# A two-block network in fp32r terms: hi and lo side by side for 512-column matmuls, modulation rows spread, first state loads moved

## The chip, the cores and the metric

The kernel runs on one core of a Trainium2 chip. It has five engines that run side by side and meet at semaphores: TensorE (matmuls, PE in the profile, its weight loads PEld), VectorE (DVE), ScalarE (ACT), GpSimd (POOL) and SyncE (SP), which here issues the transfers of the weights. Matmuls write PSUM, eight banks of 512 fp32 columns on 128 partitions. The metric is the device time of one execution in microseconds (us); less is better.

## The reference, cut to what matters

Two blocks over 256 positions of width 2048. The first has adaptive norms (a modulation of six times 2048 values, from c), a token mixer and a feed-forward part; the second has a sliding window attention, a state space model and a merge.

```python
mod = (silu(c) @ ada_w + ada_b)            # sh1, sc1, g1, sh2, sc2, g2
h = rmsnorm(x, norm1_g) * (1 + sc1) + sh1
z = h @ w_in                               # q, 6 x kv, gates, lx, ly, ga, gb
o_a = nsa_attention(...)                   # compressed, selected, window
o_b = gelu(ly) * rg_lru(causal_dwconv(lx))
merged = sigmoid(ga) * (o_a @ proj_a) + sigmoid(gb) * (o_b @ proj_b)
x = x + g1 * (merged @ w_out)
h = rmsnorm(x, norm2_g) * (1 + sc2) + sh2
gate, val = split(h @ ffn_up)
x = x + g2 * ((gelu(causal_dwconv(gate)) * val) @ ffn_down)
x = rmsnorm(x, final_g)
# second block: h @ w_in_2 -> attention, s5_ssm, glu; merged @ w_out_2, added to x
```

All of it is fp32 to begin with. The big products are made of three fp32r terms.

## The kernel before

**Groups and units.** The work of TensorE is a list of groups (`groups()`), each a product of an input with 512 columns of a weight: kc, vc, k, v, gates, q, lx, ly, then four times ga, gb, pa, pb, then wout, and for each half of the feed-forward part six gate and val and four down; behind these the groups of the second block (q2, kv2, u2, ag2, z2, ga2, pa2, gs2, gluA, gluB, ps2, wout2). A group has two units per slot, eight in most, twelve in down. A unit is a load of 2 x 128 weight rows by 512 columns, 512 KB.

**Terms.** Each input lies in SBUF as hi (rounded to fp32r) and lo (the rest), made by `put_pair`: all of hi, and all of lo behind it. For each unit ScalarE rounds the weights into whi (L1267) and VectorE writes the rest over the raw ones as wlo (L1272). TensorE then makes, for each of two rows and four output blocks, three matmuls of 256 columns into pairs[g % 2] (L1792): whi with hi, whi with lo, wlo with hi. Groups of mode N (v) swap the roles, with 512 columns (L1798).

**PSUM.** Two pairs of two banks take the groups in turn; four more banks (bank, states_in) belong to the mixers. When a group is done `evac` takes its pair out, and gives it back with the semaphore freed; the group after next waits for it.

**Order.** Every engine walks the same list of units (`walk`): at unit u VectorE and ScalarE split unit u + 4 and then do the steps of the jobs that stand at u: the evacuation of the group before, and the mixers compress, nsa (attention), lru, recurrence_back, ssm_tables, make_turns, output_factors, attention2 and states. A job gives its engine steps between which it hands over by semaphores. Whatever waits on an engine holds up what is written behind it there.

**Modulation rows.** A row is 128 of the 12,288 modulation values: 1 MB of weights, which takes two of the ten places of the ring wraw, and one VectorE instruction over 2048 elements (`ada`, L1248). Rows 0 to 31 come first; the others stand behind slots of groups, as `g.ada[s]` says; the row of slot s follows the split of unit 2s + 1, which is at step u = 2s - 3 of the walk.

**Norms.** Ahead of gate0 and of q2 the pipeline is flushed and `norm2` or `last_norms` runs; `normed_rest` then makes h2 or h3 in blocks of two rows, one ahead of each unit.

**States.** The job states (from ag2(0), unit 1) has GpSimd load turns and bz (`load_turns` L1082, `load_bz` L1085) and TensorE make states_in with bz (L1097).

## Time and profile before

| | |
|---|---|
| time, median of 3 runs | 2693.28 us (2691.06 to 2696.19) |
| time of the profiled execution | 2692.64 us |
| its span, first to last instruction | 2690.9 us |
| granted TensorE clock, mean | 0.984 |
| busy: PE, PEld, DVE, ACT, POOL | 2597.1, 2505.2, 1877.7, 1107.6, 227.3 us |
| moved | 568.13 MB, mean 211 GB/s |

The profile is of one execution. A granted clock of 1.00 is 2.4 GHz, one of 0.50 is 1.2 GHz. A matmul's duration in it is its way through the array; how fast matmuls follow each other is read from their starts. Groups of rows below name a line of the kernel before, the engine, the operation, and the tile written and the tiles read.

### The profile page before, as it was taken

How to read it: one execution, taken by the hardware profiler on the slowest of the kernel's cores; microseconds unless marked ns; L12 is line 12 of the kernel's file. 1: busy time of each engine (PE TensorE's matmuls, PEld its weight loads, DVE VectorE, ACT ScalarE, POOL GpSimd, SP SyncE). 2: the span in 40 equal slices, each digit the busy share in tenths (PEclk: the TensorE clock that was granted, in tenths of full speed). 3: DMA queues.
4: the chain of work that ended last, by engine and by line, in shares of the span. 5: the costliest groups of instructions: out<-in, count | busy, mean ns of one | idle time of the engine just before them, and what ended most of it. 6: DMA issues, size and time to landing. Idle time of an engine off the chain costs nothing.

```text
span 2690.9 us, 48148 instructions
## 1 busy us (share of the span) xinstructions
PE 2597.1 (97%) x20256; PEld 2505.2 (93%) x20256; DVE 1877.7 (70%) x2519; ACT 1107.6 (41%) x1381; POOL 227.3 (8%) x190
## 2 busy tenths in 40 slices
PE   7999999989999999899999999999999999999999
PEld 5789999889999999899999999999999888899999
DVE  7865667676866674679976556654487898898563
ACT  1033456455333344444443344444444444534432
POOL 0000000000000001000466610001100000000000
PEclk9988999999999999999999999999999999999999
DMA  9974466456888886478866766665555554465664
GB/s 404 424 269 151 156 204 188 142 157 212 274 268 275 278 276 211 134 254 274 278 225 212 221 211 181 183 185 180 165 181 180 157 162 132 149 189 176 195 197 134
DMA packets 243462, 568.13 MB, mean 211 GB/s; under 512 B 17424, under 2 KB 21520, under 8 KB 228784
## 3 DMA queue, kind: packets, MB, share of 16 engines
q1 hardware_dynamic: 233776, 530.33, 60.9%
q0 software_dynamic: 9472, 34.74, 3.6%
q8 instruction: 160, 2.62, 0.4%
q14 instruction: 54, 0.44, 0.1%
HBM read 550.85 MB, written 14.16 MB: 210 GB/s over the span
## 4 chain that ended last, share of the span: by engine, by line
PE 75%; DVE 12%; DVEq 4%; DMA 3%; ACT 3%; issue 2%; SPq 0%; ACTq 0%; POOL 0%
PE pair L1792 65%; DVE wlo L1272 4%; DMA wraw<-ada_wT_dram 3%; ACT whi L1267 2%; DVE wraw L1248 1%; PE pair L1365 1%; PE bank L499 1%; PE pair L1798 1%; DVEq L338 1%; PE pair L1785 1%; PE states_in L684 1%; PE bank L1365 1%; PE states_in L1370 1%; PE states_in L1097 0%; PE pair L1803 0%
## 5 line engine op out<-in xcount | busy, mean ns | idle before, releaser
L1272 DVE TENSOR_TENSOR wlo<-wraw,whi 128x1024 fp32r<-128x1024 f32 x777 | 977.6, 1267 | 586.0 <-ACT whi L1267 559.5
L1267 ACT ACTIVATE whi<-wraw 128x1024 fp32r<-128x1024 f32 x777 | 813.4, 1057 | 1163.9 <-PE pair L1792 669.7
L1792 PE MATMUL pair<-h_hi,whi 128*128 128x256 f32 x3936 | 1136.3, 289 | 22.2 <-DVE h_lo L426 9.2
L1792 PE MATMUL pair<-h_lo,whi 128*128 128x256 f32 x3936 | 1121.5, 285 | 0.0
L1792 PE MATMUL pair<-h_hi,wlo 128*128 128x256 f32 x3936 | 1120.8, 285 | 0.0
L1792 PEld LDWEIGHTS pair<-h_hi,whi 128*128 128x128 f32 x3936 | 763.6, 194 | 41.5 <-issue 34.9
L1792 PEld LDWEIGHTS pair<-h_lo,whi 128*128 128x128 f32 x3936 | 763.9, 194 | 0.6
L1792 PEld LDWEIGHTS pair<-h_hi,wlo 128*128 128x128 f32 x3936 | 763.1, 194 | 0.0
L1248 DVE SCALAR_TENSOR_TENSOR wraw<-wraw,cb 128x2048 f32<-128x2048 f32 x96 | 221.4, 2309 | 58.1 <-DMA wraw<-ada_wT_dram 56.8
L1792 PE MATMUL pair<-hid_hi,whi 128*128 128x256 f32 x768 | 218.5, 284 | 0.0
L1792 PE MATMUL pair<-hid_hi,wlo 128*128 128x256 f32 x768 | 217.3, 283 | 0.0
L1792 PE MATMUL pair<-hid_lo,whi 128*128 128x256 f32 x768 | 217.3, 283 | 0.0
L1792 PEld LDWEIGHTS pair<-hid_lo,whi 128*128 128x128 f32 x768 | 147.4, 192 | 0.2
L1792 PEld LDWEIGHTS pair<-hid_hi,whi 128*128 128x128 f32 x768 | 147.4, 192 | 0.2
L1792 PEld LDWEIGHTS pair<-hid_hi,wlo 128*128 128x128 f32 x768 | 147.4, 192 | 0.0
L1792 PE MATMUL pair<-m_hi,whi 128*128 128x256 f32 x512 | 145.5, 284 | 0.0
L1792 PE MATMUL pair<-m_lo,whi 128*128 128x256 f32 x512 | 144.9, 283 | 0.0
L1792 PE MATMUL pair<-m_hi,wlo 128*128 128x256 f32 x512 | 144.9, 283 | 0.0
L1792 PEld LDWEIGHTS pair<-m_lo,whi 128*128 128x128 f32 x512 | 98.3, 192 | 0.1
L1792 PEld LDWEIGHTS pair<-m_hi,whi 128*128 128x128 f32 x512 | 98.3, 192 | 0.1
L1792 PEld LDWEIGHTS pair<-m_hi,wlo 128*128 128x128 f32 x512 | 98.3, 192 | 0.0
L1365 PEld LDWEIGHTS pair<-h_f,wfour 128*128 128x128 f32 x256 | 49.1, 195 | 29.0 <-issue 22.6
(443 smaller groups left out, 3296.5 us busy)
## 6 DMA issues: line engine op xcount, KB each, us to landing
wraw<-w_in_dram SPq DMA_DIRECT2D x312, 512.0 KB, 3.7
wraw<-ada_wT_dram SPq DMA_DIRECT2D x96, 1024.0 KB, 5.8
wraw<-ffn_up_dram SPq DMA_DIRECT2D x192, 512.0 KB, 3.7
wraw<-ffn_down_dram SPq DMA_DIRECT2D x96, 512.0 KB, 4.6
wraw<-w_out_dram SPq DMA_DIRECT2D x64, 512.0 KB, 4.6
wfour<-w_in_dram SPq DMA_DIRECT2D x16, 1024.0 KB, 13.5
wraw<-proj_a_dram SPq DMA_DIRECT2D x32, 512.0 KB, 5.3
wraw<-proj_b_dram SPq DMA_DIRECT2D x32, 512.0 KB, 4.9
```

The costliest lines, as they stand in the source:

```text
L338: return ve.drain() if self.me == "dve" else None
L499: ins = te.matmul(bank[1][:, 0, 0:60], wcmp[which][:, l, :], blocks[:, l, :], start=(l == 0), stop=(l == 31))
L684: te.matmul(bank[3][:, 0, :], vv(br, 0), pt[:, br, 0:T], start=False, stop=False, skip_group_check=True)
L1248: ve.scalar_tensor_tensor(out=row, in0=row, scalar=1.0, in1=cb[:, :], op0=ALU.mult, op1=ALU.mult, accum_out=mod[:, col:col + 1]).then_inc( ...
L1267: sc.activation(whi[:, r, 0:w], wraw[:, PLACE[z], 0:w], ACT.Copy).then_inc(hi_ready, 1)
L1272: ve.tensor_tensor(wlo[:, PLACE[z], 0:w], wraw[:, PLACE[z], 0:w], whi[:, r, 0:w].bitcast(F32), ALU.subtract).then_inc(lo_ready, 1)
L1365: ins = te.matmul(out, w[:, g * CB + o * P:g * CB + (o + 1) * P], x, start=(c == 0 and o % 2 == 0), stop=(c == DC - 1), skip_group_check=True)
L1370: ins = te.matmul(flat(bank[2 + b][:, :, :]), x[:, b * P:(b + 1) * P], w[:, 3 * CB:4 * CB], start=(c == 0), stop=(c == DC - 1))
L1785: ins = te.matmul(pair[:, 2 * b, 0:48], x[:, b * P:(b + 1) * P], w[:, k * 48:(k + 1) * 48], start=(k == 0 and t == 0), stop=(k == 15 and t ...
L1792: ins = te.matmul(pair[:, o, :], w[:, at_w + o * P:at_w + (o + 1) * P], x, start=(k == 0 and o % 2 == 0 and t == 0), stop=(k == last and t ...
L1798: ins = te.matmul(flat(pair[:, 2 * b:2 * b + 2, :]), x[:, b * P:(b + 1) * P], w[:, at_w:at_w + CB], start=(k == 0 and t == 0), stop=(k == ...
```

## The change

- `put_pair` puts hi and lo of each row of 256 next to each other, so that a row of both is 512 columns. The parts are still to be had apart.
- The eight PSUM banks are now two sets of four (wides); pairs[n] is the first half of set n, the mixers' banks are the other halves.
- 41 groups are marked wide: from pb0 to down3 of the first half, without the wout groups, and gate0 to val5 of the second half. In a wide group TensorE makes, for each row and output block, one matmul of whi with 512 columns (hi and lo) into a whole bank and one of wlo with hi into its first 256 columns.
- The evacuation of a wide group begins with a ScalarE copy of the second halves into a new tile tl and a VectorE add of the first halves; what follows reads tl and not PSUM. For gates made by ScalarE alone, those who need them wait for ScalarE's semaphore.
- Modulation rows: the four of k1 and v1 go to unit pair 3 of lx0 to lx3. Of the sixteen in gate1 to val4 of the first half (two in each), four go to wout0 (two), wout1 and wout2, and twelve are one each, at slot 2, in gate0 to val5.
- A job first_turns loads the first two turns and bz in q2's first group; the job states no longer does.
- ctmp and ob_f lie elsewhere, and the last part of the recurrence is split from lr.

```diff
     def put_pair(name, at, n):
-        return put(name + "_hi", at, [P, n, T], F32R), put(name + "_lo", at + n * 1024, [P, n, T], F32R)
+        both = put(name, at, [P, n, 2, T], F32R)
+        return both[:, :, 0, :], both[:, :, 1, :], both
...
-    at = [(out[of(kind, 1)], s) for kind in ("k", "v") for s in (1, 3)]
-    at += [(out[of("q", i)], 1) for i in range(4)] + [(out[of(kind, i)], 1) for i in range(4) for kind in ("lx", "ly")]
+    at = [(out[of("q", i)], 1) for i in range(4)] + [(out[of("ly", i)], 1) for i in range(4)]
+    at += [(out[of("lx", i)], s) for i in range(4) for s in (1, 3)]
...
-    at = [(out[of(kind, i)], s) for i in range(1, 5) for kind in ("gate", "val") for s in (1, 3)]
+    at = [(out[of("wout", i)], s) for i, s in ((0, 1), (0, 3), (1, 1), (2, 1))]
+    at += [(out[of(kind, i)], 2) for i in range(6) for kind in ("gate", "val")]
...
+    for g in range(of("pb", 0), of("down", 3, 0) + 1):
+        out[g].wide = out[g].kind != "wout"
+    for g in range(of("gate", 0, 1), of("val", 5, 1) + 1):
+        out[g].wide = True
...
-    pairs = [ctx.enter_context(nc.psum_tensor(f"pair{n}", [P, 4, T], F32)) for n in range(2)]
+    wides = [ctx.enter_context(nc.psum_tensor(f"banks{n}", [P, 4, 2, T], F32)) for n in range(2)]
+    pairs = [w[:, 0:2, :, :].rearrange("p b c t -> p (b c) t") for w in wides]
...
+    def first_turns(j):
+        j.sync("to_pool", "dve", "pool", j.drained())
+        if j.me == "pool":
+            po.wait_ge(pe_units, U1[of("down", 3, 1)])
+            po.wait_ge(turns_out, 256)
+            for n in range(2):
+                load_bz(n)
+                load_turns(n)
+        yield
...
+        if gr.wide:
+            e, w = tl, wides[g % 2]
+            yield from j.hand("to_act", "dve", "act", j.drained())
+            if computed("act"):
+                ins = sc.activation(tl[:, :, :], w[:, :, 1, :], ACT.Copy)
+            yield from j.hand("act_to_dve", "act", "dve", ins)
+            if me == "dve":
+                done(ve.tensor_tensor(tl[:, :, :], w[:, :, 0, :], tl[:, :, :], ALU.add))
+                ve.drain()
+            done = lambda ins: ins
...
+    job(first_turns, start_of("q2", 0) + 2)
     job(states, start_of("ag2", 0) + 1, end_of("gs2", 3) - 2)
...
+                if gr.wide:
+                    for o in range(4):
+                        out, cols = wides[g % 2][:, o, :, :], slice(at_w + o * P, at_w + (o + 1) * P)
+                        te.matmul(out, wh[:, cols], X[gr.x][2][:, k, :, :], start=(k == 0), stop=(k == last),
+                                  skip_group_check=True)
+                        ins = te.matmul(out[:, 0, :], wl[:, cols], hi[:, k, :], start=False, stop=(k == last),
+                                        skip_group_check=True)
```

VectorE behind the prologue, where k1 is split and the first compress is prepared. L1272 is the split, L1248 a modulation row, L490 the additions that fill blocks. Before:

```order
L1272 TENSOR_TENSOR wlo<-wraw,whi 128x1024 x2
L1248 SCALAR_TENSOR_TENSOR wraw,mod<-wraw,cb 128x2048
L1272 TENSOR_TENSOR wlo<-wraw,whi 128x1024
L1416 COPY k_71<-bank 128x512 x2
L1416 COPY v_72<-states_in 128x512 x2
L1272 TENSOR_TENSOR wlo<-wraw,whi 128x1024 x3
L1248 SCALAR_TENSOR_TENSOR wraw,mod<-wraw,cb 128x2048
L490 TENSOR_SCALAR blocks<-kc_73,vec 128x60 x8
```

And now (the split is L1290, the additions L502):

```order
L1290 TENSOR_TENSOR wlo<-wraw,whi 128x1024 x3
L1446 COPY k_64<-banks 128x512 x2
L1446 COPY v_65<-banks 128x512 x2
L1290 TENSOR_TENSOR wlo<-wraw,whi 128x1024 x3
L502 TENSOR_SCALAR blocks<-kc_66,vec 128x60 x8
```

Two rows are gone from ahead of the additions; the splits and copies stand in the same order.

VectorE at the start of gate0 of the first half, where the second norm is applied block by block (L403 and L426; a split between them). Before:

```order
L1272 TENSOR_TENSOR wlo<-wraw,whi 128x1024
L403 SCALAR_TENSOR_TENSOR t_70<-res,scA,rstd 128x256 x2
L426 SCALAR_TENSOR_TENSOR h_lo<-t_70,mod,h_hi 128x256 x2
L1272 TENSOR_TENSOR wlo<-wraw,whi 128x1024
L403 SCALAR_TENSOR_TENSOR t_69<-res,scA,rstd 128x256 x2
```

And now (L415, L438; a modulation row is L1266):

```order
L1290 TENSOR_TENSOR wlo<-wraw,whi 128x1024
L415 SCALAR_TENSOR_TENSOR t_63<-res,scA,rstd 128x256 x2
L438 SCALAR_TENSOR_TENSOR h_53<-t_63,mod,h_53 128x256 x2
L1290 TENSOR_TENSOR wlo<-wraw,whi 128x1024
L1266 SCALAR_TENSOR_TENSOR wraw,mod<-wraw,cb 128x2048
L415 SCALAR_TENSOR_TENSOR t_62<-res,scA,rstd 128x256 x2
```

A modulation row stands between the second split and the third block.

GpSimd at the start of the second block. Before:

```order
L1612 DMA outT_dram<-res 128x16x256
L1082 DMA turns_101<-turns_scratch 128x1024
L1085 DMA bz<-B_dram 128x256
L1082 DMA turns_102<-turns_scratch 128x1024
L1085 DMA bz<-B_dram 128x256
```

And now:

```order
L1098 DMA bz<-B_dram 128x256
L1095 DMA turns_94<-turns_scratch 128x1024
L1098 DMA bz<-B_dram 128x256
L1095 DMA turns_95<-turns_scratch 128x1024
L1648 DMA outT_dram<-res 128x16x256
```

The four loads stand ahead of the store of outT, bz first.

## Rows read from the trace of the kernel before

**Rows 1.** The page, part 1 (busy time, share, instructions) and part 4 (chain, by engine).

```profile
PE 2597.1 (97%) x20256; PEld 2505.2 (93%) x20256; DVE 1877.7 (70%) x2519; ACT 1107.6 (41%) x1381; POOL 227.3 (8%) x190
...
PE 75%; DVE 12%; DVEq 4%; DMA 3%; ACT 3%; issue 2%; SPq 0%; ACTq 0%; POOL 0%
```

**Rows 2.** Windows: length, busy PE, PEld, DVE, ACT, POOL, PEclk, DMA share, GB/s.

```profile
700.00:1000.00 300.00, 300.00 (x2502) 300.00 (x2502) 202.94 (x175) 115.89 (x112) 0.00 (x0) 1.00 0.82 274
...
1291.50:1317.60 26.10, 23.50 (x195) 23.15 (x193) 25.15 (x28) 8.48 (x8) 11.17 (x7) 1.00 0.74 247
...
1340.70:1386.80 46.10, 46.10 (x387) 46.10 (x386) 36.38 (x30) 19.76 (x21) 32.01 (x20) 1.00 0.73 236
```

**Rows 3.** Timeline of PE in down3, 256 columns: start, duration, what.

```profile
1499.80 0.28 PE L1792 MATMUL pair<-hid_hi,whi 128*128 128x256 f32 x1
...
1507.96 0.28 PE L1792 MATMUL pair<-hid_hi,wlo 128*128 128x256 f32 x1
```

**Rows 4.** Timeline of PE in v1, 512 columns.

```profile
195.36 0.39 PE L1798 MATMUL pair<-whi,h_hi 128*128 128x512 f32 x1
...
199.90 0.39 PE L1798 MATMUL pair<-wlo,h_hi 128*128 128x512 f32 x1
```

**Rows 5.** Groups of DVE (700:1000, then 1317:1400): count, busy, mean ns; ScalarE's timeline.

```profile
L1248 DVE SCALAR_TENSOR_TENSOR wraw<-wraw,cb 128x2048 f32<-128x2048 f32 x26 | 59.6, 2292 | 41.0 <-DMA wraw<-ada_wT_dram 40.8
L1452 DVE TENSOR_TENSOR res<-t,pair 128x1024 f32<-128x1024 f32 x4 | 4.9, 1215 | 0.0
...
L1272 DVE TENSOR_TENSOR wlo<-wraw,whi 128x1024 fp32r<-128x1024 f32 x34 | 53.0, 1588 | 10.9 <-ACT whi L1267 10.0
...
2030.43 1.01 ACT L1429 ACTIVATE u<-pair 128x1024 f32<-128x1024 f32 x1
```

**Rows 6.** The first compress: timelines of DVE and PE, pieces of the chain, windows.

```profile
159.62 2.29 DVE L1248 SCALAR_TENSOR_TENSOR wraw<-wraw,cb 128x2048 f32<-128x2048 f32 x1
...
171.24 1.11 PE L499 MATMUL bank<-blocks,wcmp 128*128 128x60 f32 x4 [3.57 <-DVEq L338]
...
171.24 13.91 PE bank L499 x64
185.15 6.70 PE pair L1798 x24
...
234.29 7.09 PE bank L499 x64
...
171.00:187.00 16.00, 15.76 (x69) 15.37 (x70) 7.71 (x8) 2.18 (x3) 0.00 (x0) 0.50 0.01 5
...
234.00:242.00 8.00, 8.00 (x74) 8.00 (x73) 0.00 (x0) 0.58 (x2) 0.00 (x0) 1.00 0.60 215
```

**Rows 7.** The first states: a piece of the chain, the timeline of PE, a window.

```profile
2032.69 5.42 DMA bz<-B_dram
...
2038.25 2.08 PE L1097 MATMUL states_in<-u,bz 32*128 32x256 f32 x8 [3.13 <-DMA bz<-B_dram]
...
2038.00:2044.00 6.00, 5.75 (x25) 5.03 (x26) 3.43 (x5) 0.00 (x0) 0.00 (x0) 0.50 0.36 143
```

**Rows 8.** Timeline of PE in gate4 of the first half.

```profile
1311.12 0.36 PE L1792 MATMUL pair<-h_hi,whi 128*128 128x256 f32 x1 [2.15 <-DVE wlo L1272]
```

**Rows 9.** Timelines of DVE and PE in gate0 of the first half.

```profile
1105.37 1.22 DVE L1272 TENSOR_TENSOR wlo<-wraw,whi 128x1024 fp32r<-128x1024 f32 x1 [0.95 <-ACT whi L1267]
...
1109.34 1.23 DVE L1272 TENSOR_TENSOR wlo<-wraw,whi 128x1024 fp32r<-128x1024 f32 x1 [0.95 <-ACT whi L1267]
...
1116.38 0.39 PE L1792 MATMUL pair<-h_hi,whi 128*128 128x256 f32 x1 [0.62 <-DVE h_lo L426]
```

**Rows 10.** Timelines of DVE in lx1 and of PE in q3 and lx3.

```profile
399.62 0.42 DVE L346 CAST oa_hi<-states_in 128x256 fp32r<-128x256 f32 x1 [3.79 <-PE bank L598]
...
469.67 0.39 PE L584 MATMUL bank<-ident,pc 128*15 128x128 f32 x2 [2.31 <-DVE pc L575]
...
568.21 0.39 PE L584 MATMUL bank<-ident,pc 128*15 128x128 f32 x2 [0.18 <-DVE pc L575]
```

More of the change, by code:

```diff
@@ L50, in __init__ @@
         self.flush = False
+        self.wide = False
 def groups():
@@ L154, in build_program @@
     q4 = (put("q4a", z2 + 20 * K, [P, 4, T]), put("q4b", z2 + 24 * K, [P, 4, T]))
-    ob_f = put("ob_f", z2 + 16 * K, [P, DC, T])
+    ob_f = put("ob_f", z2 + 20 * K, [P, 12, T])
     lr = put("lr", rM, [P, 4, T])
@@ L216, in build_program @@
     b1 = put("b1", off, [P, DC])
-    ctmp = put("ctmp", off, [P, 4, 256])
+    ctmp = put("ctmp", z1 + 28 * K, [P, 4, 256])
+    tl = put("tl", off, [P, 4, T])
     bz = put("bz", off, [P, 2, 2, P])
@@ L782, in recurrence_back @@
                     j.eng.wait_ge(lru_in, 48)
-                ins = split(ob, 4 * b, 4, ob_f[:, 4 * b:4 * b + 4, :])
+                if b == 3:
+                    ve.drain()
+                ins = split(ob, 4 * b, 4, ob_f[:, 4 * b:4 * b + 4, :] if b < 3 else lr[:, :, :])
             j.ready["ob"].append(j.give("to_pe", "dve", ins))
@@ L1115, in state_outputs @@
         return j.give("pe_to_dve", "pe", ins)
+    def first_turns(j):
[7 more added lines that the diff above has]
+        yield
     def states(j):
         me, ins = j.me, None
-        j.sync("to_pool", "dve", "pool", j.drained())
-        if me == "pool":
-            po.wait_ge(turns_out, 256)
-            for n in range(2):
-                load_turns(n)
-                load_bz(n)
         if me == "dve":
@@ L1428, in evac @@
                 dst, src = ends()
-                done(sc.activation(dst, src, f))
+                ins = done(sc.activation(dst, src, f))
+            if gr.wide:
+                j.ready[k] = j.give("act_to_dve", "act", ins)
         elif k in ("lx", "gate"):
@@ L1448, in evac @@
         elif k == "pa":
-            if me == "dve":
+            if GR[of("ga", i)].wide:
+                j.take("act_to_dve", "dve", j.ready["ga"])
+            elif me == "dve":
                 j.eng.wait_ge(*evacuated("ga", i))
@@ L1454, in evac @@
         elif k == "pb":
-            if me == "dve":
+            if GR[of("gb", i)].wide:
+                j.take("act_to_dve", "dve", j.ready["gb"])
+            elif me == "dve":
                 j.eng.wait_ge(*evacuated("gb", i))
@@ L1788, in unit @@
                 k, at_w = 2 * n + kk, kk * CB
-                if "T" in gr.mode:
+                if gr.wide:
+                    for o in range(4):
[4 more added lines that the diff above has]
+                                        skip_group_check=True)
+                elif "T" in gr.mode:
                     for o in range(4 if gr.mode == "T" else 2):
```

15 lines of the change are left out of this document (7 added, 8 removed).

## The prediction, made before the changed kernel ran

> **What bounds the kernel now.** I read the page's busy table and its chain first: TensorE is busy for 97% of the span and holds 75% of the chain [rows 1]. A busy TensorE need not be at its peak, so next come the stretches: from 700 to 1000 us it never pauses, at full clock, while VectorE works 203 of 300 us and ScalarE 116 [rows 2]. The timeline then gives the pace there. From 1499.80 to 1507.96 us lie 68 starts of 256-column matmuls, 8.16 / 68 = 0.120 us each [rows 3]; a unit (two rows of 128 weights, four output blocks, three terms: 24 matmuls) takes 2.88 us. In the blocks pb0 to pb3 and gate1 to val3 of the first half, in the downs and in the whole second half, every unit takes exactly that, so whatever the change saves on TensorE there reaches the end, unless another engine's work then comes last.
>
> The rest of the time goes in places of a few us each: a wait and a slow clock near 170 us [rows 6], the mixers from 254 to 622 us, the two norms, one stall at 1309 us [rows 8], the first states at 2035 us [rows 7]. The change touches five of them.
>
> **The wide matmuls.** Thirteen groups from pb0 to pb3 (104 units), twelve gate and val groups and four downs of the first half (96 + 48) and twelve gate and val groups of the second (96): 344 units. In each unit eight triples (hi, lo, and hi with the low weights: 3 x 256 columns) become eight pairs, one 512-column matmul over hi and lo and one of 256 columns. The columns are the same, 768; one matmul and one weight load fewer. The trace has 512-column matmuls of the same type in v1: 20 starts from 195.36 to 199.90 us, 0.227 us each [rows 4]. A triple costs 0.360, a pair 0.227 + 0.120 = 0.347, so 0.013 us x 8 x 344 = 36 us. Nothing in v1 mixes the two widths, so 30 to 38 goes into the range.
>
> The rows put 256 further columns at 0.227 - 0.120 = 0.107 us, so each matmul has 0.013 us beyond its columns, and that is what one matmul fewer saves [rows 3, 4]. The Trainium skill speaks against the size of this ("TensorE: Matmul & The Clock Gate", Back-to-back issue gap): the gap is N/2.4 + 2.5 ns, so a matmul fewer would bring 2.5 ns, an estimate of 7 us for the 2752 pairs, and the sum would end at 2671. The trace does not agree: 0.120 us for 256 columns, not 0.109.
>
> What the wide form adds: per group a ScalarE copy of 1024 elements out of PSUM, 1.01 us, and a VectorE add from PSUM of 1.22 us [rows 5]; 41 groups, 41 and 50 us. They lie beside the matmuls. From 700 to 1000 us VectorE has 15.6 us of work per group of 23; it becomes 16.8 in 22.2. The pair of banks is given back two units into the next group and is wanted six units later. No group is short of cover except where ssm_tables and make_turns run.
>
> **That tight stretch.** From 1291.5 to 1317.6 us (gate4) VectorE is busy 25.2 of 26.1 us and TensorE stands 2.15 us for a split weight (the group takes 26.1 instead of 8 x 2.88 = 23.0, 3.0 us more) [rows 2, 8]. The change takes one modulation row of two out of each group from gate1 to val4 (2.3 us [rows 5], more while GpSimd works) and adds 1.2 us, so VectorE gains 1.1 us a group where TensorE is faster by 0.85: over the seven groups to gate4 some 2 to 4 us of lead more, as much as the stall. I count 3.0 us gained. In gate5 and val5 it goes the other way: split subtracts take 1.59 us there because GpSimd is busy, against 1.23 elsewhere [rows 5, 9]; two rows at 2.3 x 1.59 / 1.23 = 3.0 and two adds make 36.4 + 6.0 + 2.4 = 44.8 us of work for 44.4 us [rows 2]. That lasts two groups; the bounds are -3 and +6 us.
>
> **The first modulation rows.** k1 and v1 lose their four rows. Now the row at 159.62 us, which waited for a transfer, stands ahead of the 32 block additions; TensorE starts on them at 171.24 us, after 3.57 us idle [rows 6]. Behind that the clock stands at 0.50 from 171 to 187 us: the 64 compress matmuls take 13.91 us, and the same 64 later, at clock 1.00, take 7.09 [rows 6]. The next 24 matmuls of v1 take 6.70 instead of 24 x 0.227 = 5.45. Without the two rows ahead of them (2 x 2.3 us of VectorE, and their transfers) the additions are ready 4.6 us sooner, at 166.6, and TensorE wants them at 171.24 - 3.57 = 167.67. Then the clock should hold, as it does in the second compress, where nothing is waited for. Sum 3.57 + 6.82 + 1.25 = 11.6. Bounds: 3, if the clock falls all the same, and 13, if the first units of v1 get their weights sooner too.
>
> Four rows go to the second half of the groups lx0 to lx3 (steps at unit 3). In lx1 VectorE waits 3.79 us for TensorE right behind that place [rows 10]; the same wait stands in lx0 and lx2, and each covers a row of 2.3. In lx3 there is no such wait: the row stands ahead of the compressed scores, for which TensorE waits 0.18 us now [rows 10], and 2.5 us then. In q3 the same step, behind such a row, waits 2.31 us [rows 10]. I take +3, bounds 0 and 9.2 (four rows uncovered).
>
> **The rows of the feed-forward.** Four go to wout0 to wout2, where TensorE leads by nothing and VectorE has half its time free: nothing. One goes into gate0, where the second norm is still being applied: VectorE and ScalarE hand blocks over in steps of 3.97 us (the splits at 1105.37 and 1109.34 us) and TensorE already waits 0.62 us for h_lo [rows 9]. 2.3 us in that chain come through whole, and an idle time of 3 us stands before a low clock elsewhere [rows 6, 7]: +3.5, bounds 2 and 5. GpSimd's load of cz waits for the last row, now val5's; nobody wants cz before the third gate group of the second half, over 200 us later.
>
> **The states' first loads.** GpSimd issues turns and bz at 2032 us, behind a drain of VectorE; bz lands 5.42 us after its issue and TensorE idles 3.13 us, then runs 6.0 us at clock 0.50 with 5.75 busy [rows 7]. In the new order they are issued in q2's first group, ahead of the spill, a whole group and more sooner. The idle time goes, and about half of the 5.75: -6.0, bounds -3.1 and -6.5. The spill of outT comes behind them on GpSimd's queue, which costs it the issue of four transfers, some 2 us, with tens of us to spare. What is late next is the state chain itself, unchanged.
>
> **Costs I set at nothing.** hi and lo now interleave (rows of 256, 1 KB apart): casts and ScalarE writes have a strided target. If the cast lost its fast form it would cost VectorE half a microsecond in a dozen groups, under cover. The mixers' banks are the other half of the same eight and are not used in the wide blocks. The number of bytes is unchanged; 274 GB/s becomes 284.
>
> **The sum** against the profiled execution, 2692.6 us (its median differs by 0.6): -36 - 3 - 11.6 + 3 + 3.5 - 6 = -50.1, so 2642.5.
>
> **The rivals.**
> 1. The clock falls at the first compress all the same, or the additions stay late: -3 for -11.6, 2651. For: the estimate of 166.6 leaves 1 us of margin. Against: both causes of the delay leave.
> 2. VectorE becomes the bound between val3 and down0: GpSimd's port use stretches the convolution, which now reads SBUF instead of PSUM, and the stall grows from 3 to 9: 2651 (with the rest as forecast).
> 3. A wide matmul between two narrow ones also pays for the weight load that it hides, 0.010 us more than in v1: the pair 0.357, 0.003 x 2752 = 8 for 36, 2670.5. Against it: in v1 and in the narrow blocks each matmul pays 0.013 whatever its width [rows 3, 4]. The page's rule above would end at the same time.
> 4. The change does not do what it says: a 512-column matmul next to a 256 one takes two of 256: no gain from 344 units, 2678.5.
> 5. Slower: alternating widths uncovers a weight load. In v1 each load hides under 512 columns and elsewhere under 256 with 256 ahead; a load ahead of 512 may not. The other terms bring 14.1 us, so it decides from 14.1 / 2752 = 5.1 ns over the old triple of 0.360. At 0.375 for a pair it is 2692.6 - 14.1 + 2752 x 0.015 = 2720. Nothing in the trace points to it.
>
> **How the numbers follow.** Forecast 0.60; rivals 0.15, 0.10, 0.07, 0.04 and 0.02, and 0.02 for other things near no change. Predicted 2642.5. The low end is everything at its good bound, 38 + 13 + 6.5 + 3 - 2 = 58.5: 2634, and I go to 2632. The high end takes in rivals 1 and 2 together, 2660, and stops short of 3 to 5. A change of 0.2% (5.4 us) is about what can be told from none. Faster 0.95, same 0.02, slower 0.03.
>
> **What would show it.** In the wide blocks pairs start every 0.347 us and a unit takes 2.77. The clock stays at 1.00 between 165 and 190 us and compress takes 7 us. No idle time ahead of the first state inputs; gate0 longer by 2 to 4 us; gate4 without a stall. A unit of 2.86 us would make the main term wrong, and a TensorE waiting for wlo in gate5 or val5 the cover.

## The result, and the profile of the changed kernel

The changed kernel takes 2673.64 us (2670.66 to 2675.44) where the kernel before takes 2693.47 in the same comparison: ratio 0.9922, interval 0.9908 to 0.9937. It is faster by 20 us, 0.8%. The forecast was 2642.5 with a range up to 2660, so the sign was right and more than half of the gain is missing. The profiled execution took 2675.05 us, 17.6 less than before's; all accounts of the changed kernel below are made between these two.

Three words are used throughout. The pace of a group is the time it takes when TensorE waits for nothing in it; what a group takes beyond that is called over pace. VectorE's lead is how far its splits are ahead of the matmuls that want them. Of the wide form, a pair is one 512-column matmul and the 256-column matmul that goes with it.

The page, busy time and the chain by engine, as [rows 1]:

```profile
PE 2571.2 (96%) x17504; PEld 2351.8 (88%) x17504; DVE 1937.4 (72%) x2560; ACT 1143.8 (43%) x1422; POOL 227.3 (9%) x190
...
PE 72%; DVE 13%; DVEq 5%; ACT 4%; issue 3%; DMA 3%; SPq 0%; ACTq 0%; POOLq 0%; POOL 0%
```

There are 2752 matmuls fewer, one for each pair, but PE's busy time is only 26 us less. VectorE has 60 us more (50 are the 41 additions, at about 1.22). Its share of the chain rose by a point, and so did the share of its sequencer (DVEq): a first sign that TensorE waits more.

**The pace.** Timeline of PE, starts of 512-column matmuls; between the rows of a pair of lines lie 48 pairs:

```profile
799.92 0.40 PE L1829 MATMUL banks<-ob,whi 128*128 128x512 f32 x1
...
816.88 0.40 PE L1829 MATMUL banks<-h,whi 128*128 128x512 f32 x1
...
1199.86 0.39 PE L1829 MATMUL banks<-h,whi 128*128 128x512 f32 x1
...
1216.50 0.39 PE L1829 MATMUL banks<-h,whi 128*128 128x512 f32 x1
```

The second stretch takes 16.64 / 48 = 0.3467 us a pair, the forecast's number. The first takes 16.96 / 48 = 0.3533, and no engine is waited for in it. A unit of eight pairs is 2.827 us instead of 2.773. Both stretches have the same columns and the same clock. The slow pace holds in pb0 to pb3, the downs of the first half and the gate and val groups of the second, 29 of the 41 wide groups, and costs 13.2 us (248 units, 0.053 us each).

**Two parts that went as forecast.** Compress, 64 matmuls at full clock (compare 13.91 us in [rows 6]), and the first states, without idle time ahead of them (3.13 us in [rows 7]):

```profile
166.05 7.25 PE L511 MATMUL banks<-blocks,wcmp 128*128 128x60 f32 x64
...
2021.02 1.14 PE L1110 MATMUL banks<-u,bz 32*128 32x256 f32 x8
```

**New idle times.** Timelines of PE in lx3, wout1, gate0, gate4 (two), gate5 and down0; in brackets the idle time ahead and what ended it:

```profile
556.24 1.89 PE L596 MATMUL banks<-ident,pc 128*15 128x128 f32 x8 [2.38 <-DVE pc L587]
...
1022.00 0.70 PE L385 MATMUL banks<-t,ones 128*128 128x256 f32 x2 [1.81 <-POOLq L379]
...
1105.65 0.50 PE L1829 MATMUL banks<-h,whi 128*128 128x512 f32 x1 [0.93 <-DVE h L438]
...
1280.28 0.47 PE L1829 MATMUL banks<-h,whi 128*128 128x512 f32 x1 [2.00 <-DVE wlo L1290]
...
1300.53 0.47 PE L1829 MATMUL banks<-h,whi 128*128 128x512 f32 x1 [2.18 <-DVE wlo L1290]
...
1333.84 0.52 PE L1829 MATMUL banks<-h,whi 128*128 128x512 f32 x1 [4.88 <-DVE wlo L1290]
...
1383.14 0.50 PE L1829 MATMUL banks<-hid,whi 128*128 128x512 f32 x1 [3.12 <-DVE wlo L1290]
```

Windows of gate4, gate5, the microseconds behind gate5's stall, and the first compress (length, busy PE, PEld, DVE, ACT, POOL, PEclk, DMA share, GB/s):

```profile
1275.30:1303.70 28.40, 23.42 (x130) 19.52 (x128) 26.24 (x40) 12.78 (x14) 11.79 (x7) 1.00 0.68 223
...
1326.00:1354.90 28.90, 24.02 (x130) 20.83 (x129) 27.40 (x22) 12.96 (x13) 20.78 (x13) 0.94 0.66 216
...
1334.00:1337.40 3.40, 3.40 (x12) 2.86 (x12) 2.95 (x2) 3.26 (x4) 2.52 (x2) 0.52 0.07 28
...
171.00:187.00 16.00, 16.00 (x83) 13.61 (x83) 6.08 (x6) 5.20 (x6) 0.00 (x0) 1.00 0.30 87
```

gate4 had 3 us over its pace before [rows 8] and has 6.2 now; gate5 had none and has 6.7 (4.88 idle, the rest a clock at half speed behind it); down0 has 3.3. With 0.7 in val3 and val4 that is 16.9. What VectorE does ahead of gate5's stall, its timeline and its groups from 1303 to 1400 us:

```profile
1323.75 8.59 DVE L810 SCALAR_TENSOR_TENSOR t<-tl,vec,t 128x255 f32<-128x255 f32 x8
1332.47 1.23 DVE L1290 TENSOR_TENSOR wlo<-wraw,whi 128x1024 fp32r<-128x1024 f32 x1
...
L1290 DVE TENSOR_TENSOR wlo<-wraw,whi 128x1024 fp32r<-128x1024 f32 x33 | 53.7, 1657 | 6.8 <-ACT whi L1285 5.1 <-issue 0.4
L810 DVE SCALAR_TENSOR_TENSOR t<-tl,vec,t 128x255 f32<-128x255 f32 (+1 forms) x16 | 15.5, 1031 | 0.1
```

The eight steps of the convolution (L810) take 8.59 us; the split that TensorE waits for stands right behind them. From 1141 to 1275 us, with GpSimd idle, the same steps read the same tl in 0.478 us each.

**The account**, group by group from the first matmul of each. The wide units stand there with the pace of their stretch, and what their groups take over pace stands in the lines below:

| part | forecast | measured |
|---|---|---|
| 344 wide units | -36 | -23.5 |
| VectorE late, val3 to down0 (16.9 over pace, less the 3.0 of before) | -3 | +13.9 |
| first rows, compress | -11.6 | -11.8 |
| row in lx3 | +3 | +3.6 |
| row in gate0 | +3.5 | +3.0 |
| row in wout1 | 0 | +3.6 |
| first states | -6 | -5.9 |
| the rest (idle times and clock of the mixers) | 0 | -0.5 |
| sum | -50.1 | -17.6 |

### The profile page after: what moved, and what is told of

It reads as the page before. It is cut to its first block, busy times and chain, and to the rows that moved or that the text cites. A ratio compares the mean times of both kernels' runs of the same rounds, so it can differ in the third digit from the quotient of the medians.

```text
span 2673.3 us, 42843 instructions
## 1 busy us (share of the span) xinstructions
PE 2571.2 (96%) x17504; PEld 2351.8 (88%) x17504; DVE 1937.4 (72%) x2560; ACT 1143.8 (43%) x1422; POOL 227.3 (9%) x190
## 4 chain that ended last, share of the span: by engine, by line
PE 72%; DVE 13%; DVEq 5%; ACT 4%; issue 3%; DMA 3%; SPq 0%; ACTq 0%; POOLq 0%; POOL 0%
PE banks L1836 33%; PE banks L1829 19%; PE banks L1831 10%; DVE wlo L1290 5%; DMA wraw<-ada_wT_dram 2%; ACT whi L1285 2%; PE banks L1383 2%; DVEq L350 1%; PE banks L1842 1%; DVE t L810 1%; DVE wraw L1266 1%; PE banks L1822 1%; PE banks L511 1%; PE banks L720 1%; PE banks L696 1%
## 5 line engine op out<-in xcount | busy, mean ns | idle before, releaser
L1290 DVE TENSOR_TENSOR wlo<-wraw,whi 128x1024 fp32r<-128x1024 f32 x777 | 974.6, 1266 | 540.2 <-ACT whi L1285 511.6
L1836 PE MATMUL banks<-h,whi 128*128 128x256 f32 x4032 | 753.3, 288 | 8.0 <-DVE h L434 8.0
L1829 PE MATMUL banks<-h,whi 128*128 128x512 f32 x1920 | 679.3, 398 | 20.9 <-DVE h L438 10.6
L1836 PEld LDWEIGHTS banks<-h,whi 128*128 128x128 f32 x4032 | 637.5, 194 | 26.4 <-issue 22.5
L1836 PE MATMUL banks<-h,wlo 128*128 128x256 f32 x2016 | 574.1, 285 | 0.0
L1831 PE MATMUL banks<-h,wlo 128*128 128x256 f32 x1920 | 540.2, 281 | 0.0
L1829 PEld LDWEIGHTS banks<-h,whi 128*128 128x128 f32 x1920 | 362.2, 189 | 110.6 <-issue 19.3
L1836 PEld LDWEIGHTS banks<-h,wlo 128*128 128x128 f32 x2016 | 390.8, 194 | 0.0
L1831 PEld LDWEIGHTS banks<-h,wlo 128*128 128x128 f32 x1920 | 364.5, 190 | 0.0
L1266 DVE SCALAR_TENSOR_TENSOR wraw<-wraw,cb 128x2048 f32<-128x2048 f32 x96 | 223.1, 2326 | 33.7 <-DMA wraw<-ada_wT_dram 32.7
L1836 PE MATMUL banks<-hid,whi 128*128 128x256 f32 x768 | 139.6, 284 | 0.0
L1829 PE MATMUL banks<-hid,whi 128*128 128x512 f32 x384 | 135.8, 399 | 3.1 <-DVE wlo L1290 3.1
L1836 PEld LDWEIGHTS banks<-hid,whi 128*128 128x128 f32 x768 | 120.2, 192 | 0.4
L1836 PE MATMUL banks<-hid,wlo 128*128 128x256 f32 x384 | 108.7, 283 | 0.0
L1831 PE MATMUL banks<-hid,wlo 128*128 128x256 f32 x384 | 107.8, 281 | 0.0
L1836 PE MATMUL banks<-m,whi 128*128 128x256 f32 x512 | 94.3, 287 | 0.0
L1829 PEld LDWEIGHTS banks<-hid,whi 128*128 128x128 f32 x384 | 72.1, 188 | 21.4 <-DVE wlo L1290 3.4
```

The lines of the kernel that those rows point to most:

```text
L1266: ve.scalar_tensor_tensor(out=row, in0=row, scalar=1.0, in1=cb[:, :], op0=ALU.mult, op1=ALU.mult, accum_out=mod[:, col:col + 1]).then_inc( ...
L1290: ve.tensor_tensor(wlo[:, PLACE[z], 0:w], wraw[:, PLACE[z], 0:w], whi[:, r, 0:w].bitcast(F32), ALU.subtract).then_inc(lo_ready, 1)
L1829: te.matmul(out, wh[:, cols], X[gr.x][2][:, k, :, :], start=(k == 0), stop=(k == last), skip_group_check=True)
L1831: ins = te.matmul(out[:, 0, :], wl[:, cols], hi[:, k, :], start=False, stop=(k == last), skip_group_check=True)
L1836: ins = te.matmul(pair[:, o, :], w[:, at_w + o * P:at_w + (o + 1) * P], x, start=(k == 0 and o % 2 == 0 and t == 0), stop=(k == last and t ...
```

## The experiments

The theory: the wide form has two paces on TensorE, and its own work makes VectorE late where the tables (ssm_tables) and GpSimd's turns (make_turns) run. The rivals: the stretches where it is slow are slow for another reason (transfers, other engines); the delays come from the rows or the splits alone. Each quoted text below was written before its run.

### What the wide form is worth as a whole

```diff
-        out[g].wide = out[g].kind != "wout"
+        out[g].wide = False
...
-        out[g].wide = True
+        out[g].wide = False
```

> No group is wide: all the other edits stay (rows, first turns, the layout of hi and lo, the banks). It prices the wide form as a whole. By the forecast (0.105 us a unit and no stall added) it is 36 us slower than the changed kernel, 2710. By the reading of the two traces (some 250 units at 2.827 and 94 at 2.77, so 24 us saved, and some 10 us lost again as idle time and low clock in gate4, gate5 and down0) it is 12 to 16 us slower, 2686 to 2690.

Measured (n_all): 2679.07 us (2677.29 to 2682.12), 5.4 us over the changed kernel. That is even less than the 12 to 16 of the trace reading, which took 10 us for the late VectorE instead of 16.9 and left out wout1; 23.5 - 16.9 - 3.6 = 3.0 is what the account gives. Without wide groups gate4, gate5 and down0 have no idle time (23.04, 23.04 and 34.56 us), though GpSimd works there too (15.4 and 17.4 us in val4 and gate5), and wout1 takes 23.47. So all four delays need the wide form. gate0 (29.77) and lx3 (29.38) stay long without it. gate4's stall of before is gone by the moved rows alone: that is the -3 of the forecast, right for a narrow kernel.

### The convolution and GpSimd

```diff
-                done(ve.tensor_tensor(tl[:, :, :], w[:, :, 0, :], tl[:, :, :], ALU.add))
+                if k in ("gate", "val"):
+                    e = w[:, :, 0, :]
+                    ve.tensor_tensor(e, e, tl[:, :, :], ALU.add)
...
```

> In gate and val groups the sum of the two halves is written back into PSUM, and what follows (ScalarE's scaling, the convolution, the product) reads PSUM again; the other wide groups still use tl. Theory C (the stalls of gate4, gate5 and down0 come from VectorE instructions whose operands all lie in SBUF and which take 2 to 2.5 times as long while GpSimd makes the turns): the eight convolution steps take 3.4 to 4 us there instead of 8.6, gate4, gate5 and down0 lose most of their 13 us of idle time and low clock, 8 to 12 us faster than the changed kernel, 2662 to 2666. Rival D (the split subtracts alone, which stay in SBUF, hold VectorE up, or the row that stands in each group): the stalls keep over 8 of the 13 us, under 5 us faster.

Measured (f_psum): 2666.78 us (2664.3 to 2669.9), 6.9 under the changed kernel where 8 to 12 were expected; its trace has the slow pace in val0 to gate3 too, some 3 us that the changed kernel's trace does not have. gate5 takes 23.05 us instead of 28.89, down0 33.92 instead of 37.25, gate4 25.79 instead of 28.40. VectorE's groups from 1303 to 1400 us:

```profile
L1290 DVE TENSOR_TENSOR wlo<-wraw,whi 128x1024 fp32r<-128x1024 f32 x38 | 63.0, 1693 | 4.8 <-ACT whi L1285 3.0 <-issue 0.3
...
L810 DVE SCALAR_TENSOR_TENSOR t<-banks,vec,t 128x255 f32<-128x255 f32 (+1 forms) x16 | 6.6, 476 | 0.1
```

The splits are stretched as before (1693 ns), the convolution is not (476). Rival D falls for gate5 and down0; in gate4 3.6 us over the fast pace stay.

The other way round, GpSimd's products left out:

```diff
-                cmul(f4(turned[:, 0, :, :]), f4(turned[:, 1, :, :]), hi_(0), hi_(1), lo_(0), lo_(1), f4(px[:, :, :]),
+                if n == 0:
+                  cmul(f4(turned[:, 0, :, :]), f4(turned[:, 1, :, :]), hi_(0), hi_(1), lo_(0), lo_(1), f4(px[:, :, :]),
                      f4(py[:, :, :]), on=po)
```

> GpSimd's products for the turns are left out for all but the first of sixteen (their transfers stay), so part of the computation is missing; the rest is the changed kernel. Theory C (VectorE's instructions whose operands all lie in SBUF are stretched by GpSimd's work): the convolution's eight steps take 3.4 us everywhere, split subtracts 1.23, and the idle times in gate4, gate5 and down0 go: these three groups lose 12 us or more together, with the rest unchanged: about 2660. Rival (the wide form's hand-over, ScalarE's copy ahead of VectorE's add, makes VectorE late without GpSimd's help): gate4 to down0 keep more than 5 of the 13 us.

Measured (n_turns): 2657.1 us, one execution. Of the 18 us to the changed kernel's profiled one, 7.7 are not the edit's: this execution has the fast pace from down0 on. VectorE's groups in the same stretch:

```profile
L1291 DVE TENSOR_TENSOR wlo<-wraw,whi 128x1024 fp32r<-128x1024 f32 x39 | 46.9, 1223 | 22.8 <-ACT whi L1286 21.5 <-issue 0.4
...
L810 DVE SCALAR_TENSOR_TENSOR t<-tl,vec,t 128x255 f32<-128x255 f32 (+1 forms) x16 | 6.7, 478 | 0.1
```

gate5 22.19 and down0 33.28, exactly their pace: their delay is GpSimd's. gate4 still takes 29.21, 7.0 over pace, more than the 5 that the rival asks for. The one product left runs there, and the larger idle times lie beside it, but the delay begins before GpSimd's first product, which starts at 1288.53 us:

```profile
1281.11 0.47 PE L1830 MATMUL banks<-h,whi 128*128 128x512 f32 x1 [1.59 <-DVE wlo L1291]
```

So the theory holds for gate5 and down0, and gate4 stays open.

### The jobs that take the lead

```diff
-    job(ssm_tables, start_of("gate", 1), end_of("val", 3))
-    job(make_turns, end_of("val", 3), end_of("val", 3) + 2)
-    job(output_factors, start_of("gate", 2, 1), end_of("val", 3, 1))
+    job(ssm_tables, start_of("gate", 1), end_of("val", 5))
+    job(make_turns, end_of("val", 5), end_of("val", 5) + 2)
+    job(output_factors, start_of("gate", 4, 1), end_of("val", 5, 1))
```

> The changed kernel with three jobs moved and nothing else: ssm_tables spread over gate1 to val5 instead of gate1 to val3, make_turns from down0 on instead of gate4, output_factors in gate4 to val5 of the second half instead of gate2 to val3. Theory: the 15 us over pace of gate4 (6.2), gate5 (6.7) and down0 (3.3) come from these two jobs meeting the wide form's additional work on VectorE, first its lead eaten before gate4, then GpSimd's stretch of the convolution. In the downs VectorE has 24 us of work in 33 and reads little from tl, so GpSimd costs nothing there: 12 to 14 us faster than the changed kernel, 2660. Rival: the stretch costs the same wherever GpSimd works; the idle times move to down0 to gate1 of the second half, 2668 or more.

Measured (s_late): 2658.36 us (2650.66 to 2665.89). From val0 to the end of the second half no wide group is over its pace. (The three delays of the changed kernel add up to 16.2 us, not to the 15 of the expectation.) Windows of gate4 and of down0, where GpSimd now works:

```profile
1277.90:1300.10 22.20, 22.20 (x130) 19.58 (x129) 19.49 (x32) 9.41 (x9) 0.00 (x0) 1.00 0.76 238
1366.70:1400.00 33.30, 33.30 (x195) 29.36 (x194) 31.71 (x30) 13.58 (x14) 21.45 (x13) 1.00 0.67 225
```

The theory holds: the delay does not follow the jobs. That rests on the groups; the times alone don't show it, since this profiled execution also has the fast pace from val0 on (see r_again below). VectorE's work in down0 is 31.7 us, not 24 as the expectation said; TensorE waits for none of it.

### The rows

```diff
-    at += [(out[of("lx", i)], s) for i in range(4) for s in (1, 3)]
+    at += [(out[of("lx", i)], s) for i in range(4) for s in (1, 3) if (i, s) != (3, 3)]
+    at.append((out[of("pb", 1)], 2))
...
-    at = [(out[of("wout", i)], s) for i, s in ((0, 1), (0, 3), (1, 1), (2, 1))]
-    at += [(out[of(kind, i)], 2) for i in range(6) for kind in ("gate", "val")]
+    at = [(out[of("wout", i)], s) for i, s in ((0, 1), (0, 3), (2, 1), (2, 3))]
+    at += [(out[of(kind, i)], 2) for i in range(6) for kind in ("gate", "val") if (kind, i) != ("gate", 0)]
+    at.append((out[of("down", 0)], 4))
```

> Against the changed kernel only modulation rows move: lx3's second row to pb1, wout1's to wout2, gate0's to the middle of down0. Theory: these three rows are what lx3 (+3.6 against the kernel before), wout1 (+3.6) and gate0 (+2.1) pay, since VectorE, or the row's transfer, is late for TensorE there: lx3 back to 27.2, wout1 to 23.5, gate0 to 27.5 us, 9 us faster, 2665. Rival: wout1's idle time comes from the transfers around it (the reload of the input, 2 MB) and moves to a neighbour: 5 to 6 us faster, 2668.

Measured (r_rows): 2668.74 us; profiled 2656.65, the three timed 2668.05 to 2671.48. By group: lx3 26.94, wout1 23.46, gate0 27.43, so 3.8 + 3.6 + 2.2 us are back. The median is the rival's number, but wout2, the neighbour that should have got longer, takes 23.47 as before: by the groups the theory holds. In the changed kernel the row of wout1 came like this (VectorE's timeline):

```profile
1010.08 2.29 DVE L1266 SCALAR_TENSOR_TENSOR wraw<-wraw,cb 128x2048 f32<-128x2048 f32 x1 [5.25 <-DMA wraw<-ada_wT_dram]
```

VectorE had time, but the row's transfer was not there; the evacuation of wout0, ScalarE's squares of it and GpSimd's sums of these stood behind it, and TensorE waited for the last (the line of wout1 above). What held the transfer up was not tried; the input's reload lies beside it. The spread of 15 us between equal kernels is the next question.

The same kernel once more (r_again):

> The same kernel as r_rows, once more. Its profiled execution took 2656.7 us with units of 2.77 from down0 to val5 of the second half; its three timed ones took 2668 to 2671. If the pace is a matter of the single execution (set where TensorE restarts, with nothing in the program that decides it), this one shows units of 2.827 in the downs and the second half, some 27 groups of them, and takes 2668 to 2671. If r_rows's rows fix the pace, it takes 2656 again.

Measured: 2655.88 us. PE's starts, 48 pairs apart, in r_rows and then in r_again:

```profile
1159.74 0.39 PE L1831 MATMUL banks<-h,whi 128*128 128x512 f32 x1
...
1176.38 0.39 PE L1831 MATMUL banks<-h,whi 128*128 128x512 f32 x1
```

```profile
1159.95 0.40 PE L1831 MATMUL banks<-h,whi 128*128 128x512 f32 x1
...
1176.91 0.40 PE L1831 MATMUL banks<-h,whi 128*128 128x512 f32 x1
...
1599.80 0.39 PE L1831 MATMUL banks<-h,whi 128*128 128x512 f32 x1
...
1616.44 0.39 PE L1831 MATMUL banks<-h,whi 128*128 128x512 f32 x1
```

From val0 to gate3 one execution has 0.3467 and the other 0.3533; from down0 on both have 0.3467. So there the pace belongs to the execution, and the program does not fix it. My expectation for the downs and the time was wrong. s_late, too, has two sorts of runs: 2650.66 and 2653.43, and 2663.29 and 2665.89. In the 240 units from gate0 on a slow pace costs 240 x 0.053 = 13 us, about the distance between the sorts; that the slow ones are of that pace is inferred, since they have no trace.

The place is not without a say, however. In all seven traces of the alternating order without a drain (after, f_psum, n_turns, s_late, r_rows, r_again, u_both) pb0 to pb3 have the slow pace, 22.61 us a group. It is the one stretch that TensorE enters straight from narrow groups, without an idle time. The stretches behind a wait came out both ways: val0 to gate3 fast in four of the seven, down1 to val5 of the second half fast in four.

### The order of wide and narrow matmuls

A drain of TensorE ahead of each wide group:

```diff
+            if gr.wide and n == 0:
+                te.drain()
```

> TensorE drains once ahead of the first matmul of each of the 41 wide groups; nothing else changes against the changed kernel. Theory A (two paces: a pair takes 0.347 or 0.353 us, and which one holds is set by how the stream was last started): the drain restarts the stream at each group, so the slow units (2.827 us, some 250 of them, from pb0 to pb3, in gate4, in down0 to down3 and in the second half) change to 2.77 in all or most groups. Each drain costs 0.1 to 0.5 us: between -13 and +5 us against the changed kernel, with the groups themselves at 22.2 us instead of 22.6. Theory B (the slow pace belongs to those stretches, because of what other engines or transfers do there): units stay at 2.827 where they were, and the kernel is 4 to 20 us slower.

Measured (p_drain): 2680.61 us, 7 over the changed kernel. Groups take 22.98 or 22.56 us in no order that I can see, with 11 of 41 near the second value; a drain costs some 0.37 us (22.98 - 22.61 and 22.56 - 22.19). ga2 to ga3, slow in every other trace, are fast here, and gate1 to val2, fast in the changed kernel's, are slow. A restart can change the pace but does not choose it. The time is theory B's, but its mechanism, a pace set by what other engines or transfers do at that place, is out; theory A has the restart right and the outcome wrong.

The four wide matmuls of a row, then its four narrow ones:

```diff
                         te.matmul(out, wh[:, cols], X[gr.x][2][:, k, :, :], start=(k == 0), stop=(k == last),
                                   skip_group_check=True)
+                    for o in range(4):
+                        out, cols = wides[g % 2][:, o, :, :], slice(at_w + o * P, at_w + (o + 1) * P)
                         ins = te.matmul(out[:, 0, :], wl[:, cols], hi[:, k, :], start=False, stop=(k == last),
```

> In a wide group each row of weights now makes its four 512-column matmuls first and then its four 256-column ones; the changed kernel alternates them. Theory A (the slow pace comes from the alternation of the two widths): same-width neighbours take 0.227 and 0.120 us as in v1 and the narrow groups, every wide unit takes 2.77, and the kernel is 13 us faster than the changed one, about 2660. Theory B (a pair takes what it takes in any order, and the pace is set by the way in): some stretches stay at 2.82 and the time is within 5 us of 2674.

Measured (p_order; below, "in fours"): 2669.42 us (2666.49 to 2676.8). Every undisturbed wide group takes 22.45 us, a unit 2.806. Starts in PE's timeline (rows of four matmuls):

```profile
800.28 1.09 PE L1829 MATMUL banks<-ob,whi 128*128 128x512 f32 x4
801.22 0.63 PE L1833 MATMUL banks<-ob,wlo 128*128 128x256 f32 x4
801.68 1.09 PE L1829 MATMUL banks<-ob,whi 128*128 128x512 f32 x4
```

Four wide ones take 0.94 us, 0.235 each (0.2325 over more of them), where v1's take 0.227; four narrow ones 0.46. Theory A had 0.227, so it is wrong in size. The time lies where theory B put it, but B's paces, set by the way in, are not there: one pace came instead of two.

Eight and eight, by the same edit over both rows of a unit:

> A wide unit makes all eight 512-column matmuls, then all eight of 256 columns; alternating in fours gave 2.806 us a unit at every place, with the 512-column ones at 0.2325 and the narrow ones at 0.118. If what is lost beyond 2.77 is paid per change of width, a quarter or half of it is left: 2.78 to 2.79, 5 us faster than with fours. If a 512-column matmul with a streamed hi and lo takes 0.2325 among its like, the unit stays at 2.80 to 2.81 and the time within 3 us of the kernel with fours, 2669.

Measured (p_eight): 2665.94 us (2664.07 to 2669.4), a unit 2.794. The eight wide ones take 0.234, 0.235, 0.229, 0.232, 0.231, 0.227, 0.226 and 0.227 us (from the starts): behind a narrow one there is a run-up. Two and two (p_two):

> Two 512-column matmuls, then two of 256. In fours and eights the first wide ones behind a narrow one take 0.229 to 0.235 us and from the sixth on 0.227, the narrow ones 0.117 to 0.120. If that run-up is the law, a unit in twos takes 2.81 to 2.83 everywhere, and the faster pace of the changed kernel (2.77) never comes. If the order has nothing to do with it, both paces show here too. 2669 to 2674 us.

Measured: 2658.30 us, and every undisturbed group 22.29 us, a unit 2.786: less than with fours and eights, against the expectation from the run-up, and one pace. So the run-up is not the whole law. The same kernel, timed (p_two_t):

> p_two again, timed. Its profiled execution showed one pace, 2.786 us a unit, in all 344 units, and took 2658.3. If twos have one pace in every execution, the timed runs lie within 4 us of that, 2656 to 2663, where the alternating form's lie up to 13 us apart (r_rows: 2656.7 profiled, 2668 to 2671 timed). If the pace of twos also changes from execution to execution, some are over 2665.

Measured: 2664.23 us (2662.3 to 2666.38), and again 22.29 in every group. One run is over 2665, which the expectation gave to a changing pace, but the trace has the one pace: the time moved for another reason. The first figure of 2658.3 was a low one; the spread of 4 us among the four is no more than that of the kernel before (5 us). What is between the two profiled executions lies in the first gates and in the clock of ga2(1) and pa2(0), outside the wide groups.

### The two parts that came as forecast

Undone together: rows in k1 and v1 again, the states' first loads in the job states.

```diff
+    at = [(out[of(kind, 1)], s) for kind in ("k", "v") for s in (1, 3)]
...
-    job(first_turns, start_of("q2", 0) + 2)
```

> Against the changed kernel two parts are undone: the four rows stand in k1 and v1 again (and lx0 to lx3 have one row each), and the job states loads the first turns and bz itself. If these parts brought what the two traces show, k1 to gates0 take 80 us again instead of 68.2 (first unit of v1 20 us, compress at clock 0.50), lx3 27 to 28 instead of 30.8, and ag2(0) 30.2 instead of 24.3. Together 12 + 6 - 3 = 15 us slower, 2688. If the gain at the start was one of the wide layout or of chance, v1 stays at 29.3 us.

Measured (u_both): 2685.73 us, one execution, 12.1 over the changed kernel's median and 10.7 over its profiled execution, where 15 were expected. v1 41.28 us (29.25), lx3 27.18 (30.77), ag2(0) 30.40 (24.29): these three came as expected, 12.0 - 3.6 + 6.1. Against them wout1 and gate4 to down0 took some 6 us less than in the changed kernel's trace, and the slow pace in val0 to val3 2.5 more. The clock of the first compress is back at half:

```profile
171.00:187.00 16.00, 16.00 (x70) 15.42 (x70) 7.70 (x7) 1.48 (x3) 0.00 (x0) 0.50 0.01 2
```

### Versions put together

The next runs join edits that were tried alone. b_one joins r_rows, f_psum and the fours.

> The three edits together: the rows moved, the sum of gate and val groups kept in PSUM, and 512-column matmuls in fours. If they add up: 9 us of rows, 8 of stalls, and 344 units at 2.806 instead of 2.827 in nearly all of them (7 us) make it 2650, 24 us under the changed kernel. If idle times only move (what VectorE gains in gate4 is wanted in down0, wout1's row is wanted in wout2), 2655 to 2660.

Measured (b_one): 2652.27 us (2651.28 to 2653.75), so nearly all adds up; gate4 keeps 4.2 us over its pace. b_two takes eights and moves two more rows:

```diff
-    at += [(out[of(kind, i)], 2) for i in range(6) for kind in ("gate", "val") if (kind, i) != ("gate", 0)]
-    at.append((out[of("down", 0)], 4))
+    at += [(out[of(kind, i)], s) for kind, i, s in (("val", 0, 2), ("gate", 1, 1), ("gate", 1, 3), ("val", 1, 1),
+                                                    ("val", 1, 3), ("gate", 2, 2), ("val", 2, 2), ("gate", 3, 2),
+                                                    ("val", 4, 2), ("gate", 5, 2), ("val", 5, 2), ("down", 0, 4))]
```

> The best of before with two differences: the 512-column matmuls of a unit come in one run of eight (as in p_eight), and of the feed-forward rows the two of val3 and gate4 go to gate1 and val1, where VectorE is 11 us ahead of TensorE and has nothing better to do. Units at 2.794 instead of 2.806 bring 344 x 0.012 = 4 us; gate4 took 26.7 us, 4.2 over its 22.45, since VectorE comes into it with under 1 us of lead. If the lead that two rows (2.3 and 3.1 us) take is what is missing there, gate4 falls to about 23 us and the whole to 2644. Rival (the steps of ssm_tables and GpSimd's start make the delay in gate4 by themselves): gate4 keeps 3 us or more, 2648.

Measured (b_two): 2648.1 us (2645.87 to 2653.03), the rival's number, by another way. gate4 falls to 22.93 as the theory had it, but gate2, val2, gate3 and val3, which kept their pace in b_one, now have 4.4 us over it: the lead was spent earlier. That led to s_late. b_three joins s_late, f_psum, r_rows and twos.

> The jobs moved as in s_late, the sum of gate and val kept in PSUM, the rows of r_rows, and 512-column matmuls in twos (22.29 us a group in p_two, against 22.35 in eights). b_two still had 5.9 us over pace between gate2 and val5; they should go, and twos give 344 x 0.008 = 2.8 us: 2640. If GpSimd's work makes new idle times in the downs: 2644 to 2650.

Measured (b_three): 2643.44 us (2642.0 to 2643.71), ratio 0.9814 (0.9799 to 0.9829), 3 us over what was expected. From val0 to val5 of the second half nothing is over pace. And b_three with no group wide:

> b_three with no group wide: the same rows, the same places of the three jobs, all 344 units in narrow triples. It prices the wide form where its work on VectorE is covered and its pace is steady. b_three's units take 2.786 us against 2.88, so 344 x 0.094 = 32 us, and no idle time should differ: 2676. If the wide form had a further cost or gain outside its units, the difference is not 32 us: in the changed kernel it was worth 5 (n_all 2679 against 2674).

Measured (n_three): 2675.69 us (2673.82 to 2677.37). The wide form is worth 32.2 us there, 344 x 0.094, against 5.4 in the changed kernel. So where VectorE is in time and the pace is one, the wide form costs nothing further outside its units.

## Why the prediction was wrong, point by point

- **What bounds the kernel**: right. Where TensorE never paused, what its pace saved came out at the end. ("The whole second half" was too much: its downs 1 and 2 took 35.41 us for 34.56 before the change, and after it. They are not wide.)
- **The wide matmuls**, 0.013 us a pair: the term was mis-sized. The forecast priced a pair at 0.347 everywhere, from the rows of v1 and down3 [rows 3, 4]; in the changed kernel's trace under a third of the groups had that, and 29 of 41 ran at 0.3533, so 23.5 us came for 36. Even that was in part luck of the execution: r_again and f_psum have val0 to gate3 slow, which the changed kernel's trace has fast. v1 shows widths that don't alternate, and the forecast took a sum of two paces for the pace of a mixture. Its bounds, 30 to 38, came from no mixed row, since there was none; the lower one should have gone further down. Rival 3 had this mechanism in kind (a mixture dearer than its parts) with a pair at 0.357 and a chance of 0.07. The Trainium skill ("TensorE: Matmul & The Clock Gate", Back-to-back issue gap) gives N/2.4 + 2.5 ns as the gap of an isolated matmul and says that it is not that of a stream with weight loads; 2.5 ns for a matmul saved is an estimate of 7 us. n_three against b_three shows 32.2 / 2752 = 11.7 ns, so the runs don't bear 2.5 ns out for this stream.
- **The tight stretch**: the step that failed most, 17 us. It said that VectorE gains 1.1 us a group against 0.85 of TensorE and counted the convolution at its old price. It named the change of its operand from PSUM to SBUF only in rival 2, at 0.10, with the stall growing to 9 us; measured is 16.2 over pace in three groups, 16.9 with val3 and val4. Less the 3.0 of before that is +13.9 for -3. f_psum shows the convolution's operand to be the cause in gate5 and down0, n_turns GpSimd's products. The trace of before held both halves: beside GpSimd a split is stretched to 1588 ns [rows 5], while what reads PSUM, the convolution (L797) and the product (L1500), keeps its time. The Trainium skill says as much ("SBUF — State Buffer", Who interferes with whom): a VectorE instruction with two inputs in SBUF contends with GpSimd's reads, one with a single SBUF input outside the two-port modes does not. The traces agree: 1031 ns a step in the changed kernel against 476 in f_psum, beside the same products of GpSimd. For gate4 the cause is only known in part: its delay needs the wide form (n_all), it is gone when the tables' steps and the turns stand later (s_late), and it moves to gate2 to val3 when rows do (b_two). What share the addition, ScalarE's copy ahead of it, the tables and the first product have was not separated. VectorE's groups from 1317 to 1400 us in the kernel before, what reads PSUM:

```profile
L797 DVE SCALAR_TENSOR_TENSOR t<-pair,vec,t 128x255 f32<-128x255 f32 x8 | 3.3, 472 | 0.0
L1500 DVE TENSOR_TENSOR t<-t,pair 128x1024 f32<-128x1024 f32 x2 | 2.4, 1215 | 0.6 <-PE pair L1792 0.6
```

- **wout rows at nothing**: wrong by 3.6 us. I looked at VectorE's free time and not at the row's transfer. In the narrow n_all the same rows cost nothing, in nine other traces with wide groups and these rows (the changed kernel's 3.6 apart) wout1 has 0.5 to 4.7 us over its 23.47: how the transfer falls varies, why was not tried, and a range of 0 to 5 was due.
- **First rows, states, lx3, gate0**: right, each within 0.6 us in the traces compared. The half clock in the first compress went with the idle time ahead of it, and came back with it (u_both). lx3's 3.6 are the high end: in the traces with fours, eights and in s_late it takes 29.4, 2.2 over before.
- **Costs set at nothing** (layout, banks): right as far as shown. The cast of m takes 692 ns in both traces, and n_three, with that layout and all rows moved, is 17 us under the kernel before.
- **The range** ended at 2660 since rivals 1 and 2 were added and 3 was left out; the misses of two terms, 12.5 and 16.9 us, and the 3.6 of wout1 came together.

## What to carry to other kernels

Before a change moves an operand from PSUM to SBUF, look what the other engines do beside it: here a step of VectorE's convolution went from 476 to 1031 ns while GpSimd worked. Price a new mixture of matmuls with a bound on either side until a row shows it. Run equal kernels more than once before believing a difference: r_rows gave 2656.7 and 2671.5, and p_order, with one pace in its trace, still 2666.5 to 2676.8. Background work belongs where the engine that another waits for has lead to spare: the tables spread and the turns moved cost nothing (s_late), while rows moved from one tight place to another only moved the stall (b_two).

## What the runs showed of the hardware that I had not expected

- 512- and 256-column matmuls in strict alternation have two steady paces, 0.3467 and 0.3533 us a pair. In the eight traces with that order the pace changes only at an interruption of the stream, and behind one it differs between executions of the same program (r_rows, r_again). Entered from narrow matmuls without an interruption it was slow in all seven traces. In the fast pace the starts alternate between 0.230 and 0.117 us; in the slow one they repeat every three pairs (0.236, 0.113, 0.233, 0.117, 0.241, 0.120). In twos, fours and eights there was one pace in every profile: 0.348, 0.351 and 0.349. Why is open.
- While GpSimd multiplied in SBUF, VectorE's convolution steps took 1031 ns each from SBUF and 476 from PSUM; the additions from PSUM (1212 ns) kept their time, and the splits, all in SBUF, went from 1223 to 1657 ns.
- A drain of TensorE in a full stream costs about 0.37 us.
